# The combination of an expert pair in two parts, and a final stage in which the samples lead

## What is computed

```python
for e in range(N_EXPERTS):                        # 32 experts, each token uses 2
    a = silu(ht @ w_expert_gate[e]) * (ht @ w_expert_up[e])        # 1024 -> 512
    out = out + combine[:, e:e + 1] * (a @ w_expert_down[e])       # 512 -> 1024
x = x + out
y = x * rsqrt(mean(x * x, axis=-1) + EPS) * norm_final_g           # y_prompt, y_sample
```

## Time and profile before

| | |
|---|---|
| device time, median of 3 runs | 834.56 us (834.24 to 835.43) |
| device time of the profiled execution | 832.67 us |
| its span (first to last instruction) | 830.9 us |
| TensorE matmuls busy | 788.6 us, 95% of the span |
| VectorE, ScalarE, GpSimd busy | 247.5, 154.1, 114.2 us |
| moved by DMA | 267.99 MB, mean 323 GB/s |

### The profile page before, as it was taken

How to read it: one execution, slowest core, us unless ns; L and a number is a source line. 1 busy time by engine, 2 the same in 40 slices (tenths; PEclk the granted TensorE clock), 3 DMA queues, 4 the chain that set the end, 5 groups by cost and what they waited for, 6 DMA issues and landing times.

```text
span 830.9 us, 9590 instructions
## 1 busy us (share of the span) xinstructions
PE 788.6 (95%) x3941; PEld 455.2 (55%) x3941; DVE 247.5 (30%) x528; ACT 154.1 (19%) x242; POOL 114.2 (14%) x134
## 2 busy tenths in 40 slices
PE   6999999999999999999999999999989989999996
PEld 4888888888888888873333333333323322333332
DVE  2169957486652222361011110111011011101103
ACT  3013422434312500140111111100100110010012
POOL 5100051265620000001110000002200000000001
PEclk9999999999999999999999999999999999999999
DMA  8824656669789672379999999999999999999992
GB/s 303 251 102 164 218 166 197 181 182 202 192 280 415 242 302 102 115 263 418 427 405 429 424 427 427 427 424 429 426 430 426 428 428 425 428 421 423 421 422 108
DMA packets 73668, 267.99 MB, mean 323 GB/s; under 512 B 5518, under 2 KB 37370, under 8 KB 58255
## 3 DMA queue, kind: packets, MB, share of 16 engines
q1 hardware_dynamic: 71914, 264.34, 82.1%
q0 software_dynamic: 528, 1.90, 0.6%
q10 hardware_dynamic: 1181, 1.11, 0.4%
HBM read 259.26 MB, written 8.55 MB: 322 GB/s over the span
## 4 chain that ended last, share of the span: by engine, by line
PE 75%; DMA 15%; SPq 3%; POOL 2%; DVE 2%; issue 1%; ACT 1%; DVEq 0%; POOLq 0%
PE bank L1488 22%; PE bank L1850 19%; DMA slots<-in_w_expert_gate_dram 11%; PE bank L1888 9%; PE bank L1748 7%; PE bank L1897 5%; DMA slot<-in_w_expert_gate_dram 4%; SPq L522 3%; PE bank L1695 2%; PE bank L1531 2%; PE bank L1877 1%; DVE early L1355 1%; PE bank L1816 1%; ACT wrep L912 1%; PE bank L1578 1%
## 5 line engine op out<-in xcount | busy, mean ns | idle before, releaser
L1488 PE MATMUL bank<-hT,slots 128*128 128x264 f32 x896 | 206.7, 390 | 0.0
L1850 PE MATMUL bank<-slots,hT 128*64 128x512 f32 x688 | 192.5, 595 | 8.9 <-DMA slots<-in_w_expert_gate_dram 8.9
L1488 PEld LDWEIGHTS bank<-hT,slots 128*128 128x128 f32 x896 | 169.4, 191 | 28.8 <-issue 0.6
L1355 DVE TENSOR_TENSOR early<-early,bank 128x512 f32<-128x512 f32 x16 | 11.0, 688 | 385.7 <-PE bank L1850 385.7
L1850 PEld LDWEIGHTS bank<-slots,hT 128*64 128x64 f32 x688 | 59.4, 137 | 112.5 <-issue 98.3
L1888 PE MATMUL bank<-slots,wrep 128*64 128x512 f32 x336 | 106.4, 595 | 5.4 <-ACT wrep L912 5.4
L1850 PE MATMUL bank<-slot,hT 128*64 128x512 f32 x256 | 76.3, 594 | 2.9 <-DMA slot<-in_w_expert_gate_dram 2.9
L726 POOL COPY hT<-early 128x512 f32 x30 | 17.6, 613 | 370.1 <-PE bank L1850 286.7
L1897 PE MATMUL bank<-hT,diag 128*128 128x512 f32 x128 | 59.2, 605 | 0.2 <-ACT hT L924 0.2
L1888 PEld LDWEIGHTS bank<-slots,wrep 128*64 128x64 f32 x336 | 32.4, 137 | 47.5 <-issue 39.9
L1057 DVE SCALAR_TENSOR_TENSOR slot<-slot,rows_buf 128x256 f32<-128x256 f32 x120 | 48.1, 475 | 0.0
(11 more groups left out here) (287 smaller groups left out, 753.7 us busy)
## 6 DMA issues: line engine op xcount, KB each, us to landing
slots<-in_w_expert_down_dram SPq DMA_DIRECT2D x19, 2048.0 KB, 28.3
slots<-in_w_expert_up_dram SPq DMA_DIRECT2D x18, 2048.0 KB, 28.5
slots<-in_w_expert_gate_dram SPq DMA_DIRECT2D x18, 2048.0 KB, 28.8
slots<-in_w_in_dram SPq DMA_DIRECT2D x14, 2048.0 KB, 8.9
slot<-in_w_expert_gate_dram SPq DMA_DIRECT2D x8, 2048.0 KB, 25.8
slot<-in_w_expert_up_dram SPq DMA_DIRECT2D x5, 2048.0 KB, 26.4
slot<-in_w_expert_down_dram SPq DMA_DIRECT2D x5, 2048.0 KB, 30.9
slots<-in_w_expert_gate_dram SPq DMA_DIRECT2D x8, 1024.0 KB, 22.7
```

The source lines that it names most:

```text
L1355: dve.tensor_tensor(act.rearrange("s (f c) -> s f c", f=FT), act.rearrange("s (f c) -> s f c", f=FT), bank[UP][:, :].rearrange("s (c f) -> ...
L1488: last = mm(out, w[:, a, t * P:(t + 1) * P], hT[:, a, :], start=(a == 0), stop=(a == KT - 1))
L1850: last = mm(out[sl, :], xe[:, a, sl], expert_view(p, kind, e, a // 4)[:, a % 4, :], start=(a == 0), stop=(a == KT - 1))
```

## The change

Pairs: `combine_prompt` takes the tile t as an argument and does two of the four matmuls. In pairs 2 to 14 the first part now stands after up(p), the second part and the samples' after turn(p). In pair 15 the first part stands inside gate(15), between its steps 3 and 4 (`between` in `hidden`), and the rest after turn(15). The matmul that puts the samples' sum back moves from before down(15) to behind it.

Final stage: TensorE's order becomes tile 0 first half, samples, tile 0 second half, the sum of the samples' squares, tile 1 both halves. The samples are scaled first, and SyncE stores them before both prompt tiles. The second half of tile 1 is scaled by two engines: VectorE multiplies it with the gain row, and ScalarE multiplies that with the root (in the piece for ScalarE below). The diff, without the new semaphores' names and the two places that only serve the branch not taken:

```diff
@@ -570,11 +572,14 @@
                     sp.dma_start(g_row, ins["norm_final_g"].partition_broadcast(P)).then_inc(g_row_in, 16)
                 load_slot(n)
 
-            yp = outs["y_prompt"][0]
+            yp, ys = outs["y_prompt"][0], outs["y_sample"].rearrange("b t d -> (b t) d")
 
             def finish(k):
+                sp.wait_ge(y_sample_tok, k + 1)
+                for j in range(4):
+                    sp.dma_start(ys[:, PART * j:PART * (j + 1)], out_tok[QUART * j:QUART * j + NB, 2, 0:PART]).then_inc(y_stored, 16)
                 for t in range(2):
-                    sp.wait_ge(y_tok, 5 * k + 2 * t + 2)
+                    sp.wait_ge(y_tok, 4 * k + 2 * t + 2)
                     sp.dma_start(yp[t * P:(t + 1) * P, :], out_tok[:, t, :]).then_inc(y_stored, 16)
                 sp.wait_ge(y_stored, 96 * (k + 1))
 
@@ -741,14 +746,14 @@
                     pool.tensor_scalar(g_row, g_row, root_d, None, ALU.mult).then_inc(g_row_ready, 1)
 
             def finish(k):
+                pool.wait_ge(y_folded, k + 1)
+                pool.tensor_tensor(yrs[:, 2:3], ss[:, 2:3], power[:, :], ALU.pow).then_inc(y_sample_rstd, 1)
                 for t in range(2):
-                    pool.wait_ge(y_sq, 3 * k + t + 1)
+                    pool.wait_ge(y_sq, 2 * k + t + 1)
                     pool.tensor_scalar(ss[:, t:t + 1], ysq[:, 2 * t:2 * t + 1], ysq[:, 2 * t + 1:2 * t + 2], D * EPS,
                                        ALU.add, ALU.add).then_inc(y_ms, 1)
                     pool.wait_ge(y_ms, 2 * k + t + 1)
                     pool.tensor_tensor(yrs[:, t:t + 1], ss[:, t:t + 1], power[:, :], ALU.pow).then_inc(y_rstd, 1)
-                pool.wait_ge(y_folded, k + 1)
-                pool.tensor_tensor(yrs[:, 2:3], ss[:, 2:3], power[:, :], ALU.pow).then_inc(y_rstd, 1)
 
             finish(0)
             pool.wait_ge(flag_ready, 1)
@@ -937,20 +942,21 @@
             for p in range(PAIRS):
                 pair(p)
 
-            ys = outs["y_sample"].rearrange("b t d -> (b t) d")
-
             def finish(k):
-                for t in range(2):
-                    for i in range(2):
-                        se.wait_ge(y_sum, 5 * k + 2 * t + i + 1)
-                        last = se.activation(out_tok[:, t, CHUNK * i:CHUNK * (i + 1)], bank[Y_BANKS[t][i]][:, :], ACT.Square,
-                                             accum_out=ysq[:, 2 * t + i:2 * t + i + 1])
-                    last.then_inc(y_sq, 1)
-                se.wait_ge(y_sum, 5 * k + 5)
-                se.activation(out_tok[:, 2, 0:PART], bank[GATE][:, 0:PART], ACT.Square, accum_out=ysq[:, 4:5]).then_inc(y_sq, 1)
-                se.wait_ge(y_tok, 5 * k + 5)
-                for j in range(4):
-                    se.dma_start(ys[:, PART * j:PART * (j + 1)], out_tok[QUART * j:QUART * j + NB, 2, 0:PART]).then_inc(y_stored, 16)
+                def square(t, i, summed):
+                    se.wait_ge(y_sum, 5 * k + summed)
+                    return se.activation(out_tok[:, t, CHUNK * i:CHUNK * (i + 1)], bank[Y_BANKS[t][i]][:, :], ACT.Square,
+                                         accum_out=ysq[:, 2 * t + i:2 * t + i + 1])
+
+                square(0, 0, 1)
+                se.wait_ge(y_sum, 5 * k + 2)
+                se.activation(out_tok[:, 2, 0:PART], bank[GATE][:, 0:PART], ACT.Square, accum_out=ysq[:, 4:5]).then_inc(y_sample_sq, 1)
+                square(0, 1, 3).then_inc(y_sq, 1)
+                square(1, 0, 4)
+                square(1, 1, 5).then_inc(y_sq, 1)
+                se.wait_ge(y_rstd, 2 * k + 2)
+                se.wait_ge(y_times_g, k + 1)
+                se.activation(out_tok[:, 1, CHUNK:], out_tok[:, 1, CHUNK:], ACT.Copy, scale=yrs[:, 1:2]).then_inc(y_tok, 1)
 
             finish(0)
             se.wait_ge(flag_ready, 1)
@@ -1383,20 +1389,24 @@
             dve.tensor_copy(ytok[:, CHUNK:], bank[5][:, :]).then_inc(y_half, 1)
 
             def finish(k):
-                for t in range(2):
-                    dve.wait_ge(y_rstd, 3 * k + t + 1)
-                    if t == 0:
-                        dve.wait_ge(g_row_ready, 1)
-                    for i in range(2):
-                        part = slice(CHUNK * i, CHUNK * (i + 1))
-                        dve.scalar_tensor_tensor(out_tok[:, t, part], bank[Y_BANKS[t][i]][:, :], yrs[:, t:t + 1], g_row[:, part],
-                                                 ALU.mult, ALU.mult).then_inc(y_tok, 1)
-                    if t == 0:
-                        dve.wait_ge(y_fold, k + 1)
-                        dve.tensor_scalar(ss[:, 2:3], bank[UP][:, 0:1], D * EPS, None, ALU.add).then_inc(y_folded, 1)
-                dve.wait_ge(y_rstd, 3 * k + 3)
+                def scale(t, i):
+                    part = slice(CHUNK * i, CHUNK * (i + 1))
+                    dve.scalar_tensor_tensor(out_tok[:, t, part], bank[Y_BANKS[t][i]][:, :], yrs[:, t:t + 1], g_row[:, part],
+                                             ALU.mult, ALU.mult).then_inc(y_tok, 1)
+
+                dve.wait_ge(y_fold, k + 1)
+                dve.tensor_scalar(ss[:, 2:3], bank[UP][:, 0:1], D * EPS, None, ALU.add).then_inc(y_folded, 1)
+                dve.wait_ge(g_row_ready, 1)
+                dve.wait_ge(y_sample_rstd, k + 1)
                 dve.scalar_tensor_tensor(out_tok[:, 2, 0:PART], bank[GATE][:, 0:PART], yrs[:, 2:3], g_parts,
-                                         ALU.mult, ALU.mult).then_inc(y_tok, 1)
+                                         ALU.mult, ALU.mult).then_inc(y_sample_tok, 1)
+                dve.wait_ge(y_rstd, 2 * k + 1)
+                scale(0, 0)
+                scale(0, 1)
+                dve.wait_ge(y_sq, 2 * k + 2)
+                dve.tensor_tensor(out_tok[:, 1, CHUNK:], bank[Y_BANKS[1][1]][:, :], g_row[:, CHUNK:], ALU.mult).then_inc(y_times_g, 1)
+                dve.wait_ge(y_rstd, 2 * k + 2)
+                scale(1, 0)
 
             finish(0)
             dve.wait_ge(flag_ready, 1)
@@ -1839,8 +1849,10 @@
                         last = tr(bank[GATHER[j]][:, c * n:(c + 1) * n], xrow_by[0:n, (b - 1) % 2, 4 * j + c, :], ident[0:n, 0:n])
                     last.then_inc(m_gathered, 1)
 
-            def hidden(p, kind, out, done):
+            def hidden(p, kind, out, done, between=None):
                 for a in range(KT):
+                    if between and a == KT // 2:
+                        between()
                     for e in range(2):
                         if a % 4 == 0:
                             expert_wait(pe, p, kind, e, a // 4)
@@ -1859,7 +1871,7 @@
                     pe.wait_ge(m_silu, p)
                 if p > 1:
                     pe.wait_ge(m_added, p - 1)
-                hidden(p, 0, bank[GATE], m_gate)
+                hidden(p, 0, bank[GATE], m_gate, (lambda: combine_prompt(p - 1, 0)) if p == PAIRS - 1 else None)
 
             def up(p):
                 pe.wait_ge(m_xall, 2 * min(p, len(BLOCKS) - 1) + 2)
@@ -1903,12 +1915,11 @@
                               tile_position=(0, QUART * j))
                 return last
 
-            def combine_prompt(p):
+            def combine_prompt(p, t):
                 pe.wait_ge(m_wc, p + 1)
                 pe.wait_ge(m_ytok, 2 * p + 2)
-                for t in range(2):
-                    for i in range(2):
-                        to_rows(p, t, i)
+                for i in range(2):
+                    to_rows(p, t, i)
 
             def combine_samples(p):
                 pe.wait_ge(m_silu, p + 2)
@@ -1920,36 +1931,41 @@
             first_block()
             for p in range(PAIRS):
                 if p == 1:
-                    combine_prompt(p - 1)
+                    combine_prompt(p - 1, 0)
+                    combine_prompt(p - 1, 1)
                 gate(p)
                 if p == 0:
                     row_numbers()
-                if p > 1:
-                    combine_prompt(p - 1)
                 up(p)
-                if p:
+                if 1 < p < PAIRS - 1:
+                    combine_prompt(p - 1, 0)
+                if p == 1:
                     combine_samples(p - 1)
                 turn(p)
+                if p > 1:
+                    combine_prompt(p - 1, 1)
+                    combine_samples(p - 1)
                 if p and p + 1 < len(BLOCKS):
                     gather(p + 1)
-                if p == PAIRS - 1:
-                    pe.wait_ge(m_added, PAIRS - 1)
-                    mm(bank[GATE][:, 0:PART], ident[:, :], sample_sum, start=True, stop=False)
                 down(p)
                 if p == 0:
                     gather(1)
 
             def finish(k):
-                for t in range(2):
+                if not k:
+                    to_rows(PAIRS - 1, 0, 0, stop=True).then_inc(y_sum, 1)
+                    pe.wait_ge(y_half, 1)
+                samples_to_rows(wc_samples, start=False, stop=True).then_inc(y_sum, 5 if k else 1)
+                if not k:
```

(16 more changed lines are left out.)

7 lines of the change are left out of this document (5 added, 2 removed).

## The result

| | before | changed |
|---|---|---|
| device time, median of 14 runs each | 834.23 us (831.96 to 837.07) | 836.13 us (833.01 to 838.48) |
| ratio | | 1.0023, 95% interval 1.0012 to 1.0033 |
| profiled execution, its span | 830.9 us | 833.9 us |

The changed kernel is 0.23% slower, which is 1.9 us with an interval of 1.0 to 2.8. The forecast was 0.8 us slower (a median of 835.4 us), called no change, in a range of 833.7 to 836.8. The range holds the time.

A forecast was written before the change was run, and what follows sets the result against it. Weight loads were taken to bound the kernel. Last pair +1.0, last store's issue +1.1 and its landing -1.3 summed to +0.8 us, from 834.56 to 835.4 us, called no change, range 833.7 to 836.8.

The forecast's parts named there:

- What bounds the kernel: Mixture-of-experts stage, 372 to 811 us: weight loads set the pace, DMA share 1.01 at 424 GB/s, TensorE close to a bound.
- I cost it at nothing: Ordinary pairs 2 to 14: TensorE saves 0.92 us each, 12 us in all, counted as zero because the weights hide it.
- The last pair, +1.0: Pair 15: up ends 0.8 us earlier, up to down takes 3.90 instead of 2.17, down ends 0.95 to 1.0 us later.
- the landings do not depend on the change: Last pair's weights: arrival times read from the old trace, up's halves at 800.5 and 805.4, down's last half at 815.3.
- The issue of the last store, +1.1: Final stage: second prompt store issued at 827.1 instead of 826.0, behind four VectorE operations of 0.705 us.
- VectorE is the last: Final stage: VectorE's last scaling, until 827.1, releases the second prompt store, with ScalarE's scaling running beside it.
- a slow ScalarE (0.7) changes nothing: Final stage: ScalarE's scaling, taken as 0.60 us, could take 0.7 without moving the second prompt store's issue.
- The landing, -1.3: End of the kernel: last prompt store, with no sample stores behind it, lands 2.9 us after issue instead of 4.2.
- The bound of 4.2: End of the kernel: upper limit in us for the last store's landing after its issue; the lower was 2.4.
- The first rival: Last store slow by itself through the engine carrying it: landing 4.2 us again, sum +2.1, median 836.6; chance 0.20.
- My own sum: Whole kernel: last pair +1.0, issue +1.1, landing -1.3 give +0.8 us, a median of 835.4; chance 0.58.
- my own line of 0.2%: Whole kernel: about 0.2%, 1.67 us, taken as what a measurement can tell from no change.

The follow-up runs named there:

- e3: Against the changed kernel: new order kept only in pairs 2 to 14, last pair and final stage as before; ratio 0.9992 to before, interval 0.9978 to 1.0006.
- g1: Changed kernel without the path for experts with over 64 tokens and its branch on all five engines; run once, last store landed in 2.6 us.
- g2: Changed kernel in which the four other engines look at the flag only after all six stores landed; ratio to before 1.0056, interval 1.0042 to 1.0071.
- f1: Changed kernel without the four sample stores; run once, no time used, last prompt store's issue to release 4.6 us.
- f2: Kernel before the change without the four sample stores; run once, no time used, last prompt store's issue to release 4.2 us.
- e4: Changed kernel with last pair's half combinations inside gate and up, samples behind up, 128x256 matmul and final stage as before; ratio 0.9992 to before.
- f4: Changed kernel with the second prompt tile stored from ScalarE's queue; run once, no time used, landing 4.5 us again.
- g3: e4 with the second prompt tile stored in two halves of 256 KB, each as soon as scaled; ratio 1.0005, interval 0.9990 to 1.0019.
- g4: g3 with the branch of the other four engines behind the stores; ratio 1.0042, interval 1.0027 to 1.0057.

## Why the prediction was right, and where it was not

**What bounds the kernel: right.** DMA share 1.01 in the stage in both kernels, and e3 shows it with the ordinary pairs alone. "I cost it at nothing" holds within what e3 can tell. That a TensorE which waits longer would also run parts of the stage at the lower clock was not in the prediction; the weights hid that too.

**The last pair, +1.0: right in sum (0.9), wrong inside.** I had gate resume near 795.6 and end at 799.45, and up wait twice, 1.0 and 1.4 us. In fact up(13) waited 2.8 us for its second half, until 746.8, and ran the next 3 us at the lower clock. Pair 14 then ran without a wait for weights, and its down ended near 792.2 and not at 789.9. The last pair's gate was late enough to need next to no wait (its first half ended at 795.8, and its last landing comes at about 796.3 by the issue at 770.25 and the 26.1 us of the earlier trace rows), so the half combination in it filled a gap of some 0.5 us and not 1.3, and up waited once:

```profile
806.27 3.65 PE L1862 MATMUL bank<-slot,hT 128*64 128x512 f32 x14 [0.67 <-DMA slot<-in_w_expert_up_dram]
```

The end came out because it hangs on up's second half alone: 3.65 for up behind the landing, and 3.8 instead of 2.17 from up to down, where I had 3.90. What precedes a landing that is waited for does not reach the end. The statement "the landings do not depend on the change" holds in this sense; the place of the waits does depend on it.

**The issue of the last store, +1.1: right in size (7.94 us behind down's end, forecast 7.9 to 8.0, or 1.0 more than before).** VectorE's chain was the limit, as worked out, but only up to its third operation, the product. The last link was ScalarE's scaling, which took 0.72 and ended 0.15 us after VectorE's. "VectorE is the last" and "a slow ScalarE (0.7) changes nothing" were thus wrong by that much. The two engines that share a scaling give little, since VectorE's product must come first.

**The landing, -1.3: wrong, it is +0.3.** This is the step that failed: "Alone, with nothing behind it, I take 2.4 + 0.5 = 2.9 for the last store". The bound of 4.2 was the right end. I had chosen 2.9 because the first prompt store ran alone, and had laid the single packets until 829.7 on the samples. They were the last packets of one engine, late behind an instruction fetch of TensorE's branch (g1, g2, and the branch's own record), and f1 and f2 show that the samples were not in it. As a price for a store with nothing beside it, 2.9 was near (2.6 to 2.7 in g1 and g2); that nothing would be beside it was the error. The first rival had the size: with its landing of 4.2 its sum was +2.1, and the measured ratio gives 1.9. It was right that one engine carried the late packets, and wrong that the store is slow by itself. That the stated range holds the time is owed to this rival, whose 836.6 stands behind its upper end. My own sum was 0.7 us below the measured median, and 1.1 of the 1.9 us are missing in it.

The Trainium skill, "DMA: Bandwidth & Descriptors", section on the anatomy of one DMA, puts a transfer at about 2.0 us besides its bytes, an estimated 3.2 us here. Its fit is for transfers issued from GpSimd, and these are issued from SyncE. The undisturbed store of g1 and g2 took 2.6 to 2.7, and the disturbed one 4.2 to 4.5. The measurement decides: the page's number lies between the two and is neither.

**The chances.** I gave 0.76 to no change and 0.19 to slower, and by my own line of 0.2% the 0.23% measured is slower. With the landing right, the sum would have been 1.0 + 1.1 + 0.3 = 2.4 us in distances, and the forecast would have been slower.

## What to carry to other kernels

Where loads set the pace, work that is moved counts only from the last landing that is waited for: put what must be done ahead of the final chain into the gaps before that landing (e4), and nothing between it and the end. Before work is put in front of a final store, follow that store's own packets: a tail of single packets on its queue says that one DMA engine is late, and the other queues in the same window can say for whom. Look then at how long each engine's branch takes, since only one of the five was dear here. Storing the samples first (f1, f2), another queue (f4) and halves (g3) did not help against a fetch of instructions that falls beside the store. TensorE's branch alone, taken earlier or later than here, was not tried.

## What the runs showed of the hardware

- A fetch of instructions counts among the packets of the DMA engines that also move the data. One packet of 16 KB on q8 took about 1 us of one engine. The 512 KB store beside it landed 4.2 us after its issue in the kernel before and 4.5 in the changed one. Without the branch it took 2.6 us, and with the branch moved behind the store 2.7 us. Why the delay (up to 1.8 us) is longer than that packet is not settled, nor why the second packet comes 0.7 us behind the end of TensorE's branch in some kernels and 2.1 in others.
- The same branch took TensorE 4.7 us in the kernel before, 3.7 in the changed one, 3.4 in g2 and 3.6 in g4, and VectorE, ScalarE and GpSimd under 0.1 us each. Taken before the stores have landed it was hidden; behind them it cost SyncE 4.1 and 4.3 us of waiting (g2, g4), where it waited 0.2 before.
- TensorE's granted clock fell to 0.50 for 3.4 us behind three of five waits of 2.7 to 2.8 us in the changed kernel, and stayed at 1.00 behind the other two and behind the one of 2.9 us before.
- ScalarE's scaling of 512 columns from SBUF by a column of factors took 0.72 us, against 0.60 for the square from PSUM.
- The stream of weights as a whole lay up to 3.7 us apart (1.5 before and 2.2 behind its place in the first profile) between executions of kernels with the same loads. That is more than any term of this case, and is the reason why single profiles can't be compared by their spans.
